# Band attention beside a recurrence: both heads of a tile in six paced steps, weights scaled before their transposes, values loaded on column halves

## The reference

```
def chunk_attention(q, k, v, bias_table):        # chunks of 64 tokens, each sees itself and 8 to the left
    idx = jnp.clip(rel, -REL_CLIP, REL_CLIP) + REL_CLIP       # REL_CLIP = 128
    bias = bias_table[:, idx]
    s = jnp.einsum('bhqd,bhkd->bhqk', q_blk, kb) * scale + bias
    s = jnp.where(valid, s, NEG_INF)
    p = jax.nn.softmax(s, axis=-1)
    return jnp.einsum('bhqk,bhkd->bhqd', p, vb)

y_a = rwkv7_mix(...) * silu(gate_a)
y_b = chunk_attention(q_b, k_b, v_b, att_bias) * silu(gate_b)
h = h + concatenate([y_a, y_b]) @ w_out
```

## Time and profile before

| | |
|---|---|
| median of 3 runs | 4378.6 us |
| the profiled execution | 4384.16 us |
| its span, first to last instruction | 4382.4 us |
| PE, DVE, ACT, POOL busy | 95%, 40%, 30%, 27% |
| mean granted clock of TensorE | 0.958 of 2.4 GHz |
| the stage of RWKV and attention | about 135 to 1096 us |

### The profile page before, as it was taken

The page is one execution under the profiler, slowest core; times in us unless marked ns, Lnnn a source line. Parts: engine busy times, 40 slices in busy tenths (PEclk is TensorE's granted clock), DMA queues, the critical chain, the costliest instruction groups (busy, mean ns, idle before and its releaser), DMA issues.

```text
span 4382.4 us, 59682 instructions
## 1 busy us (share of the span) xinstructions
PE 4164.5 (95%) x26272; PEld 3316.2 (76%) x26272; DVE 1756.9 (40%) x2920; ACT 1298.7 (30%) x2266; POOL 1173.6 (27%) x583
## 2 busy tenths in 40 slices
PE   8999999999999999989999988999988999999998
PEld 4767767575699898767576867688876988888887
DVE  2434344351324126865201575123168433232344
ACT  3222222221233224455211254212166221212133
POOL 1101011010211436764032200334101532323254
PEclk9989798898999999999999989999998999999999
DMA  2101010000311112100011100221100111111110
GB/s 86 31 2 30 1 31 2 16 2 15 107 39 38 50 39 77 34 30 29 29 46 51 39 10 8 63 84 32 41 18 4 55 68 48 49 48 48 49 49 39
DMA packets 164981, 168.72 MB, mean 38 GB/s; under 512 B 8176, under 2 KB 152432, under 8 KB 164720
## 3 DMA queue, kind: packets, MB, share of 16 engines
q1 hardware_dynamic: 164720, 164.89, 11.8%
HBM read 156.48 MB, written 8.39 MB: 38 GB/s over the span
## 4 chain that ended last, share of the span: by engine, by line
PE 78%; DVE 12%; ACT 4%; POOL 3%; issue 3%; DMA 0%; POOLq 0%; SPq 0%; DVEq 0%; ACTq 0%
PE bank L629 15%; PE bank L631 15%; PE bank L630 15%; PE bank L594 9%; PE bank L617 3%; PE bank L1105 3%; PE bank L584 2%; PE bank L892 2%; PE bank L605 2%; PE bank L878 2%; PE bank L1120 1%; PE bank L779 1%; PE bank L1271 1%; POOL H L3414 1%; PE bank L1295 1%
## 5 line engine op out<-in xcount | busy, mean ns | idle before, releaser
L629 PE MATMUL bank<-XT_r,W_r 128*128 128x512 f32 x1744 | 699.8, 401 | 8.3 <-ACT BIG L1963 1.9
L630 PE MATMUL bank<-BIG_r,W_r 128*128 128x512 f32 x1624 | 632.3, 389 | 0.0
L3356 POOL TENSOR_TENSOR W_r<-W,W_r 128x2048 fp32r<-128x2048 f32 (+1 forms) x74 | 309.2, 4178 | 757.3 <-ACT W_r L1433 757.3
L631 PE MATMUL bank<-XT_r,W_r 128*128 128x512 f32 x1232 | 480.1, 390 | 0.0
L594 PE MATMUL bank<-XT,W 128*128 128x512 f32 x928 | 417.0, 607 | 3.8 <-POOL MIX L3232 2.2
L629 PE MATMUL bank<-W_r,BIG_r 128*128 128x256 f32 (+1 forms) x1280 | 418.0, 327 | 1.2 <-DVE MIX_r L2700 0.4
L629 PEld LDWEIGHTS bank<-XT_r,W_r 128*128 128x128 f32 x1744 | 327.5, 188 | 88.1 <-issue 14.2
L631 PE MATMUL bank<-W_r,BIG_r 128*128 128x256 f32 (+1 forms) x1152 | 380.4, 330 | 0.0
L630 PEld LDWEIGHTS bank<-BIG_r,W_r 128*128 128x128 f32 x1624 | 305.0, 188 | 72.0 <-issue 10.3
L594 PEld LDWEIGHTS bank<-XT,W 128*128 128x128 f32 x928 | 177.9, 195 | 220.7 <-issue 217.0
L631 PE MATMUL bank<-W_r,MIX_r 128*128 128x256 f32 x960 | 272.1, 283 | 0.0
(11 more groups left out here) (429 smaller groups left out, 7890.7 us busy)
## 6 DMA issues: line engine op xcount, KB each, us to landing
W<-w_in SPq DMA_DIRECT2D x29, 1024.0 KB, 5.5
W<-w_in_e SPq DMA_DIRECT2D x33, 512.0 KB, 5.8
MIX<-w_up SPq DMA_DIRECT2D x15, 1024.0 KB, 5.3
MIX<-w_down SPq DMA_DIRECT2D x15, 1024.0 KB, 4.8
W<-w_in_o SPq DMA_DIRECT2D x12, 1024.0 KB, 5.0
W<-w_in SPq DMA_DIRECT2D x17, 512.0 KB, 4.2
H<-x SPq DMA_DIRECT2D x16, 512.0 KB, 9.5
W<-w_out SPq DMA_DIRECT2D x7, 1024.0 KB, 4.8
```

Of the source, the lines that this page charges most:

```text
L629: E.matmul(b[:, 0:n], lh, rh, start=k == ks[0], stop=False)
L630: E.matmul(b[:, 0:n], lh, rl, start=False, stop=False)
L631: mm = E.matmul(b[:, 0:n], ll, rh, start=False, stop=k == ks[-1])
L3356: G.tensor_tensor(WLO[k % 2][:, 0:n], WSTAGE[k % 2][:, 0:n], WHI[k % 2][:, 0:n], ALU.subtract).then_inc(*s_split.mark("split", k))
```

## The change

`pace` now takes 224 steps in 224 rounds. A tile of attention has six steps, in which both heads stand together: scores of both heads (step 0), transposes of both (step 4), value products of both (step 5). DVE adds the near bias in step 0, takes the maxima in step 1, and in step 3 takes the reciprocals and scales the probabilities themselves (new), before their transposes. ACT adds the far bias in step 0 (new, Identity with a bias), makes the exponentials in step 2 and copies in steps 4 and 5. GpSimd writes the mask of the far block into the scores (new) in place of the mask tile FAR. The fifth blocks of both heads share one transpose bank and one copy (new). The value product swaps its operands: 64 columns of V are loaded and 128 columns of probabilities streamed, head 0 into partitions 0 to 63 of a bank, head 1 into 64 to 127, in turn. The output thus comes out transposed; its scaling, its transpose and the tile O go. The 15 `KEEP_UP` entries of attention go. The output bank joins the ring, which has four banks.

```diff
-        RW_ROUNDS, BAND_STEPS = 218, 192
+        RW_ROUNDS, BAND_STEPS = 224, 224
-        for_rw, for_band, for_band_o = ring(0, 4), ring(4, 3), ring(7, 1)
+        for_rw, for_band = ring(0, 4), ring(4, 4)
-        KEEP_UP.update({("band", "p_tr", h, i, 0): n for h, i, n in ((0, 7, 8), (1, 7, 7), (2, 4, 8), (3, 7, 3), (4, 0, 3))})
...
-                {("band", "p_tr", *at, 0): n for *at, n in ((0, 4, 3), (1, 5, 6), (3, 3, 3), (2, 6, 8), (4, 4, 5), (5, 4, 8),
-                                                            (4, 5, 3), (7, 2, 2), (6, 5, 9), (7, 6, 4))},
...
 def pe_band():
+                    pe.wait_ge(*done("band", "qkv_act", c))
+                    pe.wait_ge(*done("band", "qkv_dve", c))
+                    for what, n, at in (("far", far, k0), ("near", near, k0 + far)):
+                        if n:
+                            for hl in range(2):
+                                b = for_band.open("band", what, c, i, hl)
+                                pe.wait_ge(*for_band.free("band", what, c, i, hl))
+                            for hl in range(2):
+                                pr = slice(64 * hl, 64 * hl + 64)
+                                E.matmul(for_band.bank("band", what, c, i, hl)[:, 0:n * P], QT_B[pr, i * P:(i + 1) * P],
+                                         KT_B[pr, at * P:(at + n) * P], start=True, stop=True).then_inc(
+                                             *band.pe.mark("band", what, c, i, hl))
+                    yield from nothing(4)
                     for hl in range(2):
...
+                        pe_transposes(band, for_band, ("p_tr", c, i, hl),
+                                      [S_B[hl][:, j * P:(j + 1) * P] for j in range(min(4, nk))],
+                                      done("band", "unit", c, i, hl))
+                    if nk > 4:
+                        pe_transposes(band, for_band, ("p_last", c, i), [S_B[hl][:, HALF:HALF + P] for hl in range(2)])
                     yield
-                    pe_transposes(band, for_band, ("o_tr", c, i), [O_B], done("ev", "band", "o", c, i))
+                    b = for_band.open("band", "o", c, i)
+                    pe.wait_ge(*for_band.free("band", "o", c, i))
...
+                    for j in range(nk):
+                        for hl in range(2):
+                            hs = slice(64 * hl, 64 * hl + 64)
+                            mm = E.matmul(b[hs, 0:P], VN_B[:, k0 + j, hs], PT_B[hl][:, j * P:(j + 1) * P], start=j == 0,
+                                          stop=j == nk - 1)
+                    mm.then_inc(*band.pe.mark("band", "o", c, i))
+                    yield
...
 def act_band():
+                    if far:
+                        for hl in range(2):
+                            h = 2 * c + hl
+                            act.wait_ge(*done("band", "far", c, i, hl))
+                            S.activation(S_B[hl][:, 0:far * P], for_band.bank("band", "far", c, i, hl)[:, 0:far * P],
+                                         ACT.Identity, bias=PAR[:, FAR_AT + h:FAR_AT + h + 1]).then_inc(
+                                             *band.act.mark("ev", "band", "far", c, i, hl))
+                    yield from nothing(2)
...
+                    yield from nothing(2)
+                    for hl in range(2):
+                        act_copy_out(band, for_band, ("p_tr", c, i, hl), PT_B[hl][:, 0:min(4, nk) * P], min(4, nk) * P)
                     yield
                     if i % 2:
-                        act_copy_out(band, for_band, ("o_tr", c, i), MIX[:, 4 + c, i * P:(i + 1) * P], P)
+                        act_copy_out(band, for_band, ("o", c, i), MIX[:, 4 + c, i * P:(i + 1) * P], P)
+                    yield
...
 def dve_band():
+                    yield
+                    yield
                     hs = slice(2 * c, 2 * c + 2)
-                    dve.wait_ge(*done("band", "p", 2 * c + 1, i))
+                    dve.wait_ge(*done("band", "p", c, i, 1))
                     V.reciprocal(st_b[:, 2, hs], st_b[:, 1, hs]).then_inc(*band.dve.mark())
                     dve.wait_ge(*band.dve.last())
+                    for hl in range(2):
+                        h = 2 * c + hl
+                        V.tensor_scalar(S_B[hl][:, 0:nk * P], S_B[hl][:, 0:nk * P], st_b[:, 2, h:h + 1], None,
+                                        ALU.mult).then_inc(*band.dve.mark("band", "unit", c, i, hl))
+                    yield
+                    if nk > 4:
+                        dve.wait_ge(*done("band", "p_last", c, i))
+                        V.tensor_copy(PT_LAST, for_band.bank("band", "p_last", c, i)[:, 0:Q].rearrange(
+                            "p (h n) -> p h n", h=2)).then_inc(*band.dve.mark("ev", "band", "p_last", c, i))
...
 def pool_band():
+            for c in range(4):
+                yield from nothing(6)
+                for i in range(NT):
+                    if band_keys(i)[1] == 3:
+                        for hl in range(2):
+                            pool.wait_ge(*done("ev", "band", "far", c, i, hl))
+                            G.memset(S_B[hl][64:128, 0:64], NEG).then_inc(*band.pool.mark("band", "masked", c, i, hl))
+                    yield from nothing(6)
```

More of the change, by code:

```diff
@@ L867, in pe_band @@
                     near, far, nk, k0 = band_keys(i)
-                    for hl in range(2):
[L869 to L894, removed]
@@ L2647, in dve_band @@
                     near, far, nk, k0 = band_keys(i)
+                    dve.wait_ge(*done("band", "bias"))
                     for hl in range(2):
                         h = 2 * c + hl
[L2650 to L2658 removed]
@@ L2659, in dve_band @@
-                        dve.wait_ge(*done("band", "near", h, i))
-                        V.tensor_tensor(S_B[hl][:, far * P:nk * P], for_band.bank("band", "near", h, i)[:, 0:near * P],
-                                        BIAS[:, h, (2 - near) * P:256], ALU.add).then_inc(
-                                            *band.dve.mark("ev", "band", "near", h, i))
-                        dve.wait_ge(*band.dve.last())
-                        V.tensor_reduce(st_b[:, 0, h:h + 1], S_B[hl][:, 0:nk * P], AX.X, ALU.max, negate=True).then_inc(
-                            *band.dve.mark("band", "max", h, i))
@@ new lines, in dve_band @@
+                        V.tensor_tensor(S_B[hl][:, far * P:nk * P], for_band.bank("band", "near", c, i, hl)[:, 0:near * P],
+                                        BIAS[:, h, (2 - near) * P:256], ALU.add).then_inc(
+                                            *band.dve.mark("ev", "band", "near", c, i, hl))
+                    yield
+                    for hl in range(2):
+                        h = 2 * c + hl
+                        if far:
+                            dve.wait_ge(*done("ev", "band", "far", c, i, hl))
+                        if far == 3:
+                            dve.wait_ge(*done("band", "masked", c, i, hl))
+                        dve.wait_ge(*done("ev", "band", "near", c, i, hl))
+                        V.tensor_reduce(st_b[:, 0, h:h + 1], S_B[hl][:, 0:nk * P], AX.X, ALU.max, negate=True).then_inc(
+                            *band.dve.mark("band", "max", c, i, hl))
@@ L3333, in pool_band @@
                 band.pool.note("gtmp_free", "band", "gate", half)
-            yield from nothing(4 * 46)
+            for c in range(4):
+                yield from nothing(6)
+                for i in range(NT):
+                    if band_keys(i)[1] == 3:
+                        for hl in range(2):
+                            pool.wait_ge(*done("ev", "band", "far", c, i, hl))
+                            G.memset(S_B[hl][64:128, 0:64], NEG).then_inc(*band.pool.mark("band", "masked", c, i, hl))
+                    yield from nothing(6)
             yield from pool_gate_T(band, "gate", lambda ct, half: half_of(MIX[:, 4 + ct, :], half),
-                                   lambda ct, half: done("ev", "band", "o_tr", 3, NT - 2))
+                                   lambda ct, half: done("ev", "band", "o", 3, NT - 2))
         def pool_even():
```

54 lines of the change are left out of this document (16 added, 38 removed).

## The result

The changed kernel took **4251.6 us**, the median of four runs (4241.2 to 4255.2), beside 4378.1 (4376.2 to 4380.3) for the kernel before: a ratio of 0.971, 95% interval 0.969 to 0.973. The forecast was 4319 us in a range from 4268 to 4364. The direction was right. The gain of 127 us is twice the 60 forecast and lies outside the range. The profiled execution took 4255.23 us against 4384.16, 128.9 less.

A forecast was written before the change was run, and what follows sets the result against it. TensorE (PE), busy 95% of the span, was taken as the bound: -91 PE work, +19 moved steps and +12 waits gave -60 against 4384.2, so 4324, or 4319 us against the median, range 4268 to 4364.

The forecast's parts named there:

- PE work: Attention tiles: scores, values and output save 2.8 us per tile, 67 us at full clock over 24 tiles.
- Scores: Score products of two heads on row halves, taken as half overlapping: 1.3 us instead of 2.5, saving 1.2 per tile.
- Values: Value products on alternating column halves, two at a time, 0.055 us a pass: 1.1 us, saving 1.4 per tile.
- The keep-ups: Attention's 160 identity passes, 18 us at full clock, fill a wait: removal counted at nothing, up to 18 us more possible.
- The clock: Two-generator stage: some 36% of the attention work runs at half speed, so the 67 us saved times 1.36 gives 91.
- moved steps: Cold tails: 7 state steps and 7/3 tiles lose the full clock they had beside wide products, 11 + 8, +19 us.
- Rival 1: Tails: denser work lets the clock reach 2.4 GHz for half their time, 4278 us; chance 0.15.
- Waits: PE's 36.6 us of waiting for the exponential before the transposes grows by a third, +12 us.
- rival 4: Both heads' exponentials and maxima delay state and factor operations by 1 us per tile more: 4345 to 4350; chance 0.10.
- Rival 2: Weaves: the clock falls with less PE work and no keep-ups; three cold give +120, 4440 us; chance 0.07.
- Rival 3: Attention products: the halves do not overlap, 4355 us, or 4389 by the skill's weight-load rule; chance 0.13.
- my signs: Right if tail steps near 5.5 us at clock 0.5 to 0.6, weaves near 45; wrong if tails mostly at full clock.

The follow-up runs named there:

- both packings undone: Changed kernel with head 1's scores one round after head 0's and the old value operands, output left untransposed, new spacing kept: 4293.1 us, 0.981.
- the last kernel: Kernel before with only attention's order changed (six steps, heads' scores in steps 0 and 1, transposes in 3 and 4, values in 5), keep-ups kept: 4276.5 us, 0.9755.

## Why the prediction was wrong

The direction and the place were right, the work nearly so, the clock was not.

- **PE work, forecast 67 us at full clock plus keep-ups at nothing: measured 76.** Scores: forecast 29 (24 x 1.2), measured 21 to 23. Values: 34 (24 x 1.4), measured 20 to 22. A tile of 20 value passes takes 1.25 us with its change of shape, against the forecast 1.1, and 0.055 us from pass to pass within as forecast. The two together give 50 to 52. The output's transposes were forecast at 5; with the bias of the work column taken out 7 are left for them. The keep-ups are 26 (23), which I set at nothing; the kernel without them shows what replaced them, 7.5 of idle and 34 of cold time. So the 76 stand near the forecast 67 in part by luck: the products were forecast more than 10 too high and the keep-ups missing.
- **The clock, forecast as a factor of 1.36 on the saving (-24 us) and +19 for moved steps, in all -5: measured -60 (-55 with the bias taken out). This is the step that failed.** I held the tails at half clock as a given state of the stage, and read from them only what work costs there. But the state depended on the order, which the change also changed. Three runs show that: one round less distance gives +65 us of cold time and +36 of idle; both packings undone with the distance kept leaves 55 cold; and the order alone, in the kernel before, takes cold time from 201 to 27. My account of how: PE stood still once per head, for 1.3 us in the cold tail, and a cold spell, once begun, lasted as long as that pattern did. With four rounds between scores and transposes a slow PE has its own state steps to do while the chain of additions, maximum, exponential and scaling runs. While cold it hardly stands still (3.5 us in the stage, 13.1 before), and the clock comes back within 3.4 to 6.8 us. The lengths of the spells speak for it, at most 6.8 us after and 54.6 before, with about as much idle time in all. One stretch of the kernel before speaks against it as the whole cause (behind this list).
- **Rival 1 (chance 0.15) was the event, at too small a size.** It let the tails be warm for half their time, where their clock of 0.78 to 0.84 means 56 to 68%, and gave 4278. Taken apart as the table is, it has work -67, clock -34 (the 24 and 29 less the 19) and idle 0, against -76, -60 and +4. It argued with denser work. The same work in the new order has the least cold time, and both packings undone is no colder than the change itself, so the denser products are not it. It also kept the moved steps' price.
- **Moved steps, +19: nothing that shows.** An empty sixth step in the kernel before costs 0.0008 of the time, 0.0018 at most. Its stage is 6 us longer, with 17 us more of cold time; why the tails bear the extra tiles and steps so cheaply was not looked into.
- **Waits, +12: +4.** The wait before the transposes fell to 12.8 us from 36.6 instead of rising, and the waits for VectorE's state came in its place (11.5), as the bursts of rival 4 would have it. Parting the two maxima halved this wait (5.7), so half of it is their burst; what makes the other half is not settled. Taking the scaling away left it at 11.5.
- **Rival 2** was true in a small way: three of four weaves ran at 0.92 of the clock, 6.8 cold us each. In the run of the same kernel once more none did.
- **Rival 3** fell: both halves overlap. The trace shows 0.055 us from one value pass to the next with all 128 rows in use, half of the 0.11 of the earlier trace rows. This disagrees with a rule of the Trainium skill, TensorE: Matmul & The Clock Gate, Part 3 (The mechanism), by which a weight load overlaps the matmuls in flight only where row groups differ.
- **Of my signs**, the pairs, the value passes, the missing transposes and the gates came as said; a weave took 40.5 to 43.5 us instead of 45, and a tail step 4.3 us (34.4 / 8) instead of 5.5, at a clock of 0.78 to 0.84, which is the sign that I had put under wrong.

**What stays argued of the clock.** The kernel before, the end of the longest cold spell of its second tail (509.1 to 539.8), columns as above:

```profile
519.30:539.80 20.50, 20.50 (x81) 15.82 (x82) 5.29 (x16) 3.47 (x10) 0.00 (x0) 0.50 0.00 1
```

PE did not wait at all in these 20.5 us and stayed at 1.2 GHz. So that the order sets the cold time is shown; that it does so through the short waits alone is argued.

**Where the gain of the new products went.** By the order alone the kernel stands at 4276.5; with the new products and without keep-ups at 4252 and 4239. That is 25 to 37 us for some 74 us less work. In the stage, against the kernel with the order alone, idle grew by 25 us and cold time by 20 to 55, worth 10 to 27. With less work on PE between the links of the same chain, the chain shows. One part of it is named: the wait of L615 for the scaling, 12.8 us, where L617 waits 0.7 for the exponential in the kernel with the order alone. Which of what differs between the two (both heads' transposes in one step, far additions on ScalarE, the keep-ups) makes the rest was not tried, nor was the new value product in the head-by-head order of the last kernel.

## What to carry to other kernels

A stretch at half clock is a symptom to be explained, not a price list: look for the short wait that repeats in it, and ask whether PE would still have to wait if it ran slowly. Where two chains are interleaved by hand, try the distance between producer and consumer before the products themselves; here it brought 103 of 127 us with the same instructions. When work is taken from the busy engine, test the order alone as its own kernel, for the gain may be the order's, and the work saved may come back as waits.

## What was not expected of the hardware

- Idle time and cold time do not go together. The kernels before and after are idle for 61.0 and 65.0 us in the stage and cold for 201 and 82; the changed kernel run again is idle for 65.2 and cold for 48. The number of cold spells is much the same, 12, 15 and 11; their length is not, at most 54.6, 6.8 and 6.8 us. The sum of the idle time says nothing on it.
- The Trainium skill, TensorE: Matmul & The Clock Gate, in Part 1 under "HAM oscillation", tells of a kernel that waits for DMA between short bursts of matmuls and is throttled each time, and advises to restructure its loop so that PE stays warm. The waits here are of 1 to 2 us and for other engines. The last kernel agrees with the advice: with the work as it was (802 us), the order took the granted clock of the stage from 0.90 to 0.98.
- Matmuls on row halves overlap although a program gives one head's first and the other's behind it: eight score passes took 1.35 us in both orders, and passes of the two halves started 7 and 13 ns apart.
- The same program on the same inputs had its cold spells in other places from one profile to the other (81.9 and 47.8 us), and its medians differed by 12 us; those of the kernel before, taken five times, lay within 8 (4372.5 to 4379.8).
